# Modulation chunks spread over later stages of a trunk layer, and head weights laid out by the host

## The reference

```python
mod = jax.nn.silu(c) @ w_ada + b_ada          # c: 1 prompt row + 8 sample rows, w_ada 1024 x 6144
sh1, sc1, g1, sh2, sc2, g2 = jnp.split(mod[:, None, :], 6, axis=-1)
h = layer_norm(x) * (1.0 + sc1) + sh1
mix, st = token_mixers(h, pos0, C0, n0, m0, S0, w_in, b_in, head_g, w_out)
x = layer_norm(ALPHA * x + g1 * mix, ln1_g, ln1_b)
h = layer_norm(x) * (1.0 + sc2) + sh2
x = layer_norm(ALPHA * x + g2 * peer(h, w_pq, sub_keys, expert_u, expert_v), ln2_g, ln2_b)
```

## Time and profile before

| | us |
|---|---|
| median of 3 runs | 3905.58 (3902.49 to 3909.03) |
| the profiled execution's own time | 3903.29 |
| its span in the trace | 3901.5 |
| modulation, up to the first load of the norm stage | 114.05 |
| norm stage, to 183.14 | 69.1 |
| gates stage, to 215.76 | 32.6 |
| heads stage with what lies behind it, to 941.8 | 726.0 |
| output stage, to about 1165 | 223 |
| the rest, to 3901.5 | 2736 |

### The profile page before, as it was taken

One profiled execution on the slowest core, in us unless ns is written; L12 is line 12 of the kernel. 1 busy time (PEld: TensorE's weight loads), 2 busy tenths in 40 slices (PEclk: granted clock), 3 DMA queues, 4 the chain that ended last, 5 costly groups with the idle time before them and its releaser, 6 DMA issues. The chain is left out here.

```text
span 3901.5 us, 46687 instructions
## 1 busy us (share of the span) xinstructions
PE 3288.4 (84%) x16909; PEld 2623.8 (67%) x16909; DVE 2914.0 (75%) x5948; ACT 993.9 (25%) x1966; POOL 1930.6 (49%) x1654
## 2 busy tenths in 40 slices
PE   7649999995857887873799999999999999999992
PEld 1525554442327886873788888888888888888881
DVE  1423333433875888887999999999999999999996
ACT  0101111112001676765222221222222222222220
POOL 0000000000110887886777767777677776776750
PEclk9579999997988898985899999999999999999996
DMA  7252133202122244245999999999999999999983
GB/s 268 84 60 36 36 36 50 58 6 93 70 89 97 54 93 90 57 87 117 387 366 376 360 367 371 363 384 359 367 374 371 380 360 367 372 376 373 355 315 140
DMA packets 456413, 874.31 MB, mean 224 GB/s; under 512 B 196317, under 2 KB 245853, under 8 KB 456038
## 3 DMA queue, kind: packets, MB, share of 16 engines
q0 software_dynamic: 153008, 555.83, 37.5%
q1 hardware_dynamic: 303176, 315.50, 27.4%
HBM read 808.07 MB, written 63.15 MB: 223 GB/s over the span
## 5 line engine op out<-in xcount | busy, mean ns | idle before, releaser
L1492 POOL DMA_INDIRECT ring<-in_expert_u,experts x512 | 724.1, 1414 | 266.0 <-issue 132.3
L1492 POOL DMA_INDIRECT ring<-in_expert_v,experts x512 | 683.7, 1335 | 290.1 <-DVE acc L1620 151.2
L1620 DVE SCALAR_TENSOR_TENSOR acc<-ring,wgt,acc 128x1024 f32<-128x1024 f32 x508 | 651.7, 1283 | 23.5
L1611 DVE CUSTOM_DVE_ANT_1 ring<-ring,h2T 128x1024 f32<-128x1024 f32 x512 | 610.4, 1224 | 21.1 <-DMA ring<-in_expert_u,experts 19.8
L1254 POOL TENSOR_SCALAR hotJ<-cst,pickT 128x128 f32<-128x128 f32 x560 | 467.0, 851 | 189.7 <-ACT pickT L1242 100.4
L672 PE MATMUL z<-W,hT 128*128 128x512 f32 x1152 | 508.5, 595 | 38.5 <-DMA bh<-in_b_in 38.5
L1508 PE MATMUL a<-h2T_hi,uhi 128*128 128x320 f32 x2048 | 349.3, 313 | 85.8 <-DVE ulo L1626 49.2
L672 PEld LDWEIGHTS z<-W,hT 128*128 128x128 f32 x1152 | 214.4, 191 | 281.6 <-issue 281.6
L1508 PEld LDWEIGHTS a<-h2T_hi,uhi 128*128 128x128 f32 x2048 | 316.4, 190 | 97.9 <-DVE ulo L1626 50.0
L1530 PE MATMUL v<-vhi,whi 128*128 128x512 f32 x768 | 305.1, 397 | 82.8 <-DVE vlo L1634 78.1
L1508 PE MATMUL a<-h2T_lo,uhi 128*128 128x320 f32 x2048 | 348.4, 313 | 0.0
(11 more groups left out here) (275 smaller groups left out, 5216.0 us busy)
## 6 DMA issues: line engine op xcount, KB each, us to landing
ub<-in_expert_uT SPq DMA_DIRECT2D x128, 512.0 KB, 6.7
vf<-in_expert_v SPq DMA_DIRECT2D x128, 512.0 KB, 9.9
weight_d<-stage SPq DMA_DIRECT2D x10, 4096.0 KB, 20.8
wt<-weight_d SPq DMA_DIRECT2D x128, 320.0 KB, 7.9
wa<-in_w_ada SPq DMA_DIRECT2D x12, 2048.0 KB, 7.9
W<-in_w_in SPq DMA_DIRECT2D x32, 512.0 KB, 9.1
wq<-in_w_pq SPq DMA_DIRECT2D x4, 2048.0 KB, 19.8
ring<-in_expert_u,experts POOLq DMA_INDIRECT x512, 7.1
```

The source lines that it names most:

```text
L1492: pool.indirect_dma_start(ring[:, r, :], None, table, bass.IndirectOffsetOnAxis(experts[:, gb, k % SLOTS:k % SLOTS + 1], 0)).then_inc(land ...
L1611: dve.tensor_tensor_reduce(u, u, h2, 1.0, 0.0, ALU.mult, ALU.add, dots[:, k:k + 1]).then_inc(used, 1)
L1620: dve.scalar_tensor_tensor(dst, src, wk, dst, ALU.mult, ALU.add).then_inc(used, 1)
```

## The change

The 12 chunks are no longer computed together. Chunks 0 to 3 (shift 1 and scale 1) precede the norm stage; 4, 5 and 6 are computed in the norm stage, 7, 8 and 9 in the gates stage, and 10 and 11 in the output stage. Each chunk has its own load (with a slice of the bias), product, take and store of 9 x 512 values by a DMA of POOL. There are two buffers instead of three, laid over `hB` and `gB`, which the heads stage fills later; in the output stage there are two of their own. The 1 of the scale parts is added in the take. c is laid out by the host as `cT`, so that silu runs on 128 x 72 and no transpose is needed. The clearing of semaphores between modulation and norm is gone.

Each head's weights lie in HBM as one piece of 16 KB for each partition, with one DMA for weights and one for bias, and those of heads 0 and 1 are issued by SP in the gates stage. `w_gates` and `w_out` are laid out in the same way. In the output stage `head_g`, `w_out` and the two ln1 rows have a semaphore each, and POOL waits for `head_g` alone.

```diff
+class Modulation:
...
+    def load(self, sp, c):
+        r, cols = c % self.NBUF, slice(c * WCOL, (c + 1) * WCOL)
+        if c >= self.NBUF:
+            sp.wait_ge(self.taken, c - self.NBUF + 1)
+        sp.dma_start(self.b9[:, r, :], self.a["b_ada"][0, cols].partition_broadcast(9)).then_inc(self.loaded[r], 16)
+        sp.dma_start(self.wa[:, r, :, :], self.a["w_ada"][0, :, cols].rearrange("(k p) n -> p k n", p=P)
+                     ).then_inc(self.loaded[r], 16)
+
+    def product(self, pe, c, bank):
...
+        pe.wait_ge(self.loaded[r], 32 * (c // self.NBUF + 1))
+        if c >= 2:
+            pe.wait_ge(self.taken, c - 1)
+        for k in range(KC):
+            mm = pe.matmul(bank, self.cT[:, k, :], self.wa[:, r, k, :], start=(k == 0), stop=(k == KC - 1))
+        mm.then_inc(self.prod_done, 1)
+
+    def take(self, dve, c, bank):
...
+        dve.wait_ge(self.prod_done, c + 1)
+        if c >= 2:
+            dve.wait_ge(self.stored[c % 2], 16 * (c // 2))
+        dve.scalar_tensor_tensor(self.out[:, c % 2, :], bank, one, self.b9[:, c % self.NBUF, :], ALU.add, ALU.add
+                                 ).then_inc(self.taken, 1)
+
+    def store(self, pool, c):
+        pool.wait_ge(self.taken, c + 1)
+        pool.dma_start(self.mod_d[:, c * WCOL:(c + 1) * WCOL], self.out[:, c % 2, :]).then_inc(self.stored[c % 2], 16)
...
+            sp.dma_start(cT[:, :, :], a["cT"]).then_inc(c_in, 16)
+            for c in range(FIRST):
+                md.load(sp, c)
...
+            for c in range(FIRST):
+                md.store(pool, c)
+            md.all_stored(pool, FIRST)
...
+    def load_head(self, sp, a, hd):
+        hh = hd % 2
+        sp.dma_start(self.W[:, hh, :, :, :], a["w_heads"][hd]).then_inc(self.w_in[hh], 16)
+        sp.dma_start(self.bh[:, hh, :, :], a["b_heads"][hd].partition_broadcast(P)).then_inc(self.w_in[hh], 16)
...
+            IN_NORM = {3: FIRST, 5: FIRST + 1, 7: FIRST + 2}
...
                     sp.dma_start(xb[:, b % NX, :], x_block(a, b)).then_inc(x_in[b % NX], 16)
+                    if b in IN_NORM:
+                        md.load(sp, IN_NORM[b])
...
                     dve.scalar_tensor_tensor(xv, xv, rs[:, b % 2, :], sh[:, :], ALU.mult, ALU.add).then_inc(h_ready, 1)
+                    if b - 1 in IN_NORM:
+                        md.take(dve, IN_NORM[b - 1], mod_bank(IN_NORM[b - 1]))
...
+                    if b in IN_NORM:
+                        md.product(pe, IN_NORM[b], mod_bank(IN_NORM[b]))
...
+            MOD = (FIRST + 3, FIRST + 4, FIRST + 5)
...
+                for c in MOD:
+                    md.store(pool, c)
+                md.all_stored(pool, MOD[-1] + 1)
...
+                for c in MOD:
+                    md.load(sp, c)
+                for hd in range(2):
+                    mix.load_head(sp, a, hd)
...
+                md.product(pe, MOD[0], mod_bank(MOD[0]))
                 pe.wait_ge(lf_ready, 1)
...
+                for c in MOD[1:]:
+                    md.product(pe, c, mod_bank(c))
                 pe.wait_ge(y_ready, 1)
...
                     dve.tensor_reduce(G["R"][:, b, :], arow[:, b % 2, :, :], AX, ALU.max).then_inc(row_taken, 1)
+                    if b == 0:
+                        md.take(dve, MOD[0], mod_bank(MOD[0]))
...
+                for c in MOD[1:]:
+                    md.take(dve, c, mod_bank(c))
                 dve.wait_ge(y_ps, 1)
...
+        LAST = {2: NCB - 2, 4: NCB - 1}
...
+            sp.dma_start(hg[:, :], a["head_g"][0].partition_broadcast(P)).then_inc(hg_in, 16)
+            sp.dma_start(wo[:, :, :], a["w_out"]).then_inc(w_in_, 16)
...
-            pool.wait_ge(w_in_, 64)
+            pool.wait_ge(hg_in, 16)
...
+                if b - 1 in LAST:
+                    md.product(pe, LAST[b - 1], mps[LAST[b - 1] % 2][:, :])
...
+                if b - 2 in LAST:
+                    md.take(dve, LAST[b - 2], mps[LAST[b - 2] % 2][:, :])
```

More of the change, by code:

```diff
@@ L165, in build @@
             cst_mix.append(mid.enter_context(nc.sbuf_tensor("cst_mix", [P, NKEEP - NLATE], F32)))
-            with semaphores(nc) as sem:
-                modulation_phase(nc, a, sem, mod_d, cst, cst_mix[0], ones, const)
             hB = mid.enter_context(nc.sbuf_tensor("hB", [P, NB, D], F32))
@@ new lines, with __init__, all_stored @@
+NCB = 6 * D // WCOL
+FIRST = 2 * D // WCOL
+class Modulation:
+    def __init__(self, nc, a, sem, mod_d, wa, cT, rows):
+        self.a, self.mod_d, self.wa, self.cT = a, mod_d, wa, cT
+        self.NBUF = wa.shape[1]
+        self.b9, self.out = rows
+        self.loaded = [sem(f"m_w{i}") for i in range(self.NBUF)]
+        self.prod_done, self.taken = sem("m_prod"), sem("m_taken")
+        self.stored = [sem(f"m_st{i}") for i in range(2)]
+    def load(self, sp, c):
[6 more added lines that the diff above has]
+    def product(self, pe, c, bank):
+        r = c % self.NBUF
+        pe.wait_ge(self.loaded[r], 32 * (c // self.NBUF + 1))
[5 more added lines that the diff above has]
+    def take(self, dve, c, bank):
+        one = 1.0 if c * WCOL // D in (1, 4) else 0.0
+        dve.wait_ge(self.prod_done, c + 1)
[6 more added lines that the diff above has]
+        pool.dma_start(self.mod_d[:, c * WCOL:(c + 1) * WCOL], self.out[:, c % 2, :]).then_inc(self.stored[c % 2], 16)
+    def all_stored(self, eng, n):
+        for i in range(2):
+            eng.wait_ge(self.stored[i], 16 * len(range(i, n, 2)))
@@ L231, in modulation_phase @@
+def modulation_phase(nc, a, sem, md, cT, cst, cst_mix, ones):
+    with ExitStack() as ctx:
+        e = ctx.enter_context(nc.sbuf_tensor("e9", [P, KC, 9], F32))
+        mps = [ctx.enter_context(nc.psum_tensor(f"mod_ps{i}", [9, WCOL], F32)) for i in range(2)]
+        c_in, cst_in, exp_done, silu_done, ones_ready = sem("m_in"), sem("m_cst"), sem("m_exp"), sem("m_silu"), sem("m_ones")
         block = ctx.enter_context(nc.Block())
@@ L381, in _ @@
                 sp.wait_ge(rows_in, 16 * (4 * SEQS + 1))
+            @block.gpsimd
+            def _(pool):
+                for c in IN_NORM.values():
+                    md.store(pool, c)
             @block.scalar
@@ L586, in heads_phase @@
         C = sb2("C", [P, 2, VW])
-        w_in_ = [sem(f"c_w{i}") for i in range(2)]
         cs_in = [sem(f"c_cs{i}") for i in range(2)]
@@ L1805 @@
     args["expert_uT"] = nc.dram_tensor("in_expert_uT", (NK, P, KC, NK), F32, kind="ExternalInput").ap()
+    w_in = np.asarray(inputs["w_in"])[0].reshape(KC, P, -1).transpose(1, 0, 2)
+    b_in = np.asarray(inputs["b_in"])[0]
+    cuts = [[(RET0 if hd // H else 0) + part * MW + hd % H * DH for part in ORDER] for hd in range(2 * H)]
+    laid = {
+        "cT": np.concatenate([inputs["c_prompt"], inputs["c_sample"]], 0).reshape(9, KC, P).transpose(2, 1, 0),
+        "w_heads": np.stack([np.stack([w_in[:, :, lo:lo + DH] for lo in cut], 2) for cut in cuts]),
+        "b_heads": np.stack([np.stack([b_in[lo:lo + DH] for lo in cut]) for cut in cuts]),
+        "w_gates": w_in[:, :, GATE0:RET0],
+        "b_gates": b_in[GATE0:RET0],
+        "w_out": np.asarray(inputs["w_out"])[0].reshape(KC, P, D).transpose(1, 0, 2),
+    }
+    for name, x in laid.items():
+        arrays[f"in_{name}"] = np.ascontiguousarray(x)
+        args[name] = nc.dram_tensor(f"in_{name}", x.shape, F32, kind="ExternalInput").ap()
     arrays["in_consts"] = constants(np)
```

142 lines of the change are left out of this document (55 added, 87 removed).

## The result

The changed kernel is faster, by 1.7 to 1.8 per cent. In the first comparison its median was 3840.8 us (3830.6 to 3849.6, 4 runs) against 3904.7 (3902.5 to 3909.0), a ratio of 0.9834 with an interval of 0.9808 to 0.986; a second one, on another occasion, gave 3830.6 (3829.8 to 3844.3, 5 runs) against 3907.0, a ratio of 0.9816 (0.9797 to 0.9835). The forecast was 3844, its range 3824 to 3862.

A forecast was written before the change was run, and what follows sets the result against it. Stages run one after another, each bound by its own engine or wait: PE in modulation and norm, a chain of small steps in gates. Terms -67 + 22.5 + 28 - 36.6 - 8.5 = -61.6 gave 3844 us against the median, range 3824 to 3862.

The forecast's parts named there:

- Modulation, -67: Modulation stage: small c load, short silu and fewer chunks let the norm stage start at 47 instead of 114 us; -62 to -69.
- the lower bound of 3: End of the modulation stage, after the last take: 4.5 us expected where 7.2 lay before, bounds 3 and 7.
- Norm, +22.5: Norm stage: chunks 4, 5 and 6 priced at 9.5 us each, samples' rows hidden behind chunk 6; +14 to +25 us.
- rival A: Norm and gates stages: clock stays up, chunks 5, 6 and 8 at 2.4 GHz; sum -72.7, 3833 us; chance 0.17.
- Rival B: Norm and gates stages: clock stays down, every product takes 13.7 us; sum -31.2, 3874 us; chance 0.06.
- Gates, +28: Gates stage: PE waits for chunk 7's load, then products of chunks 7, 8 and 9 lengthen it; +20 to +33 us.
- Heads, -36.6: Heads stage: weights of heads 0 and 1 arrive early, so PE starts 1.1 us in instead of 37.7.
- rival C: Heads stage: weights keep their old load pace of 37.7 us and come late; 3853 us; chance 0.07.
- Output, -8.5: Output stage: POOL gates earlier, less the cost of chunks 10 and 11 and their takes; -6 to -11 us.
- the split: Output stage: POOL no longer waits for the ln1 loads, so y is ready earlier; -11.5 us.
- The sum, -61.6: Whole kernel: all five stage terms together, 3841.7 against the profiled 3903.3 us, or 3844 against the median.
- The forecast's half bounds: Whole kernel: half of each term's bounds, since they do not all fall one way, said to give 3826 to 3858 us.

## Why the prediction was right, and where it was off

**Modulation, -67 against -69.0.** Step by step as put: load 0 at 9.61 (9.5), product 0's take from 18.35 (19.0), load 2 at 27.40 (28.0), the last take ended at 42.15 (42.6). The end of the stage took 2.95, just under the lower bound of 3, not 4.5. One reading doesn't come out of the trace as put: over the first product of the kernel before, the granted clock reads 1.00, although fewer passes fit into a stretch than right behind it.

```profile
24.00:26.00 2.00, 2.00 (x3) 0.28 (x2) 0.00 (x0) 0.00 (x0) 0.00 (x0) 1.00 0.42 158
26.00:28.00 2.00, 2.00 (x6) 0.46 (x5) 0.00 (x0) 0.00 (x0) 0.00 (x0) 1.00 0.00 0
```

That its first passes ran at the lower level is thus inferred from their pace, half of the later one. Products that began at a recorded 0.50 took about as long (8.8 to 9.9).

**Norm, +22.5 against +17.5: the term that was mis-sized most.** Up to chunk 6 the steps stand: product, take behind DVE's wait, next block, 19.2 us from product to product where 19.9 was worked out. The miss is behind chunk 6. There I gave the faster clock 2.5 us; the transposes and gate products ran 8.76, 0.93 and 6.48 us from the product's start to the end, 16.2, where the forecast had 9.5, 1.95 and 10.25 less 2.5, 19.2. In that last part it went nearly as rival A had it, and between chunks as the forecast had it: the clock fell back to 0.50 each time (92 to 96, 112 to 115.3), so that no product took under 8.76. In its total the stage lies between the two, nearer to A's +14. Rival B is out: no product of the changed kernel took more than 9.99 us, in the norm or the gates stage, where it put 13.7.

**Gates, +28 against +27.5.** All steps within 0.5 us (8.74 for the load, sums at 18.4, ends at 39.0, 9.84 and 7.03 for the products). That chunk 8 meets a low clock is not certain, though: in other executions it took 7.04 and the stage 55.8.

**Heads, -36.6 against -36.9.** The weights landed within the gates stage, and rival C is out. The reason was wrong in part: it was the old matrix's slices that were slow, but their 512 bytes account for little of it.

**Output, -8.5 against -9.0.** Two misses that cancel: the split gave 10.6, not 11.5, and the chunks cost 1.7, not 3.0. The forecast's own parts give less than its term, too: 11.5 less 2.2 for two products and 1.4 for two takes are 7.9, not 8.5.

**The sum, -61.6 against -69.9.** 5.0 of the difference are the norm stage, 2.0 the modulation stage, above all its end. The median of the first comparison is 64 lower than the kernel before, that of the second 76: 70 is between them, and the expert stage's scatter moves each execution by up to 17. That the first median came so close to 3844 is luck in part: the expert stage's scatter took back in the profiled execution what the stages had gained beyond the sum. By the stages alone the measured -69.9 is nearer to rival A's -72.7 than to the forecast, though A's condition, products of 6.9 us, didn't hold in the norm stage. The forecast's half bounds were worked out wrongly, too: half of each term's bounds gives 3833 to 3856, not 3826 to 3858.
